# Up projection of the expert blocks: one bank and 512-column products instead of two banks and 256-column ones, with the gating multiply behind it

## What is computed

```python
def expert_block(args):
    xb_i, e = args
    h = jax.nn.silu(xb_i @ w_gate[e]) * (xb_i @ w_up[e])
    return h @ w_down[e]
```

## Time and profile before

| | us |
|---|---|
| median of 3 runs | 2057.61 |
| lowest, highest | 2056.06, 2059.81 |
| span of the profiled execution | 2054.1 |
| TensorE busy | 1895.9 (92%) |
| VectorE busy | 1034.9 (50%) |
| ScalarE busy | 832.3 (41%) |
| GpSimd busy | 283.8 (14%) |

### The profile page before, as it was taken

How to read it: one execution, slowest core, us unless ns; L and a number is a source line. 1 busy time by engine, 2 the same in 40 slices (tenths; PEclk the granted TensorE clock), 3 DMA queues, 4 the chain that set the end, 5 groups by cost and what they waited for, 6 DMA issues and landing times. The chain is left out here.

```text
span 2054.1 us, 28746 instructions
## 1 busy us (share of the span) xinstructions
PE 1895.9 (92%) x9892; PEld 1600.8 (78%) x9893; DVE 1034.9 (50%) x2051; ACT 832.3 (41%) x1564; POOL 283.8 (14%) x388
## 2 busy tenths in 40 slices
PE   6999999999999999999997764999999999999980
PEld 5788888888878888888885543888888888888870
DVE  4644455544454544555444654454456454546434
ACT  4333333333343333333323553444446454446423
POOL 2000000010000010000100202222222222222223
PEclk9999999999999999999997886999999999999995
DMA  6332333323342223522334575585566576656428
GB/s 213 123 100 85 139 140 132 103 92 135 123 145 96 90 83 131 173 77 95 103 123 166 169 250 168 149 268 162 155 224 218 169 264 191 184 174 215 142 53 340
DMA packets 173306, 316.24 MB, mean 154 GB/s; under 512 B 9757, under 2 KB 92701, under 8 KB 173226
## 3 DMA queue, kind: packets, MB, share of 16 engines
q1 hardware_dynamic: 155754, 255.07, 36.0%
q0 software_dynamic: 15120, 51.59, 10.1%
q10 hardware_dynamic: 2352, 8.52, 1.0%
HBM read 266.09 MB, written 49.07 MB: 153 GB/s over the span
## 5 line engine op out<-in xcount | busy, mean ns | idle before, releaser
L751 DVE TENSOR_TENSOR wl<-raw,wh 128x512 fp32r<-128x512 f32 x440 | 274.3, 685 | 207.2 <-ACT wh L573 205.3
L1597 PE MATMUL bank<-gu_hi,ex_hi 128*128 128x256 f32 (+1 forms) x960 | 310.5, 323 | 4.5 <-DVE gu_lo L1507 4.5
L60 PE MATMUL bank<-xT_hi,wh 128*128 128x512 f32 x768 | 301.0, 392 | 10.6 <-ACT ext L711 7.0
L1599 PE MATMUL bank<-gu_hi,ex_lo 128*128 128x256 f32 (+1 forms) x960 | 307.1, 320 | 0.0
L1598 PE MATMUL bank<-gu_lo,ex_hi 128*128 128x256 f32 (+1 forms) x960 | 306.9, 320 | 0.0
L62 PE MATMUL bank<-xT_hi,wl 128*128 128x512 f32 x768 | 299.4, 390 | 0.0
L61 PE MATMUL bank<-xT_lo,wh 128*128 128x512 f32 x768 | 299.3, 390 | 0.0
L573 ACT ACTIVATE wh<-raw 128x512 fp32r<-128x512 f32 x440 | 240.2, 619 | 99.5 <-PE bank L1140 49.9
L1597 PEld LDWEIGHTS bank<-gu_hi,ex_hi 128*128 128x128 f32 x960 | 183.2, 191 | 23.9 <-DVE gu_lo L1507 6.5
L1599 PEld LDWEIGHTS bank<-gu_hi,ex_lo 128*128 128x128 f32 x960 | 183.2, 191 | 13.3
L1598 PEld LDWEIGHTS bank<-gu_lo,ex_hi 128*128 128x128 f32 x960 | 183.5, 191 | 12.5
(11 more groups left out here) (239 smaller groups left out, 3258.0 us busy)
## 6 DMA issues: line engine op xcount, KB each, us to landing
raw<-in_w_in SPq DMA_DIRECT2D x70, 1024.0 KB
raw_gate_up<-in_w_gate SPq DMA_DIRECT2D x16, 2048.0 KB, 8.4
raw_gate_up<-in_w_up SPq DMA_DIRECT2D x16, 2048.0 KB, 13.4
raw_d<-in_w_down SPq DMA_DIRECT2D x16, 2048.0 KB, 13.0
raw<-in_w_out SPq DMA_DIRECT2D x20, 1024.0 KB
raw<-in_w_up_pool SPq DMA_DIRECT2D x20, 512.0 KB
raw<-in_w_up_gmlp SPq DMA_DIRECT2D x20, 512.0 KB
h<-in_x_prompt SPq DMA_DIRECT2D x16, 512.0 KB, 5.2
```

Of the source, the lines that this page charges most:

```text
L60: nc.tensor.matmul(out, lh, rh, start=(i == 0), stop=False)
L751: lo = lambda out, x, hi: tt(out, x, hi.bitcast(F32), ALU.subtract)
L1597: nc.tensor.matmul(out, a[0][:, ka, :], w[0][:, kw, cols], start=(n == 0), stop=False)
L1599: return nc.tensor.matmul(out, a[1][:, ka, :], w[0][:, kw, cols], start=False, stop=(n == total - 1))
```

## The change

The up projection goes into one bank (`bankU` is bank 1) with matmuls of 512 columns, in the same form as the gate projection. `u1_done` is gone. VectorE waits for `gu_done`, the end of the whole up projection, and then multiplies both halves of the hidden rows one behind the other. The first pair of transposes of the hidden rows moves behind the transposes of x. The second pair writes to bank 2, which is free now, instead of bank 0.

```diff
-    bankG, bankU, bankY = psum[0], psum[1:3], psum[3:5]
-    bankX, bankH = psum[5:7], [psum[7], psum[0]]
+    bankG, bankU, bankY = psum[0], psum[1], psum[3:5]
+    bankX, bankH = psum[5:7], [psum[7], psum[2]]
@@ VectorE, per_block
-                    dve.wait_ge(u1_done, j + 1)
-                    tt(hid[:, 0:256], bankU[0][:, 0:256], sg[:, 0:256], ALU.mult).then_inc(hid_ok, 1)
+                    dve.wait_ge(gu_done, j + 2)
+                    tt(hid[:, 0:256], bankU[:, 0:256], sg[:, 0:256], ALU.mult).then_inc(hid_ok, 1)
+                    tt(hid[:, 256:512], bankU[:, 256:512], sg[:, 256:512], ALU.mult).then_inc(hid_ok, 1)
                     down(0)
                     dve.wait_ge(hT_hi, 2 * j + 1)
                     hidden_low(0)
-                    dve.wait_ge(gu_done, j + 2)
-                    tt(hid[:, 256:512], bankU[1][:, 0:256], sg[:, 256:512], ALU.mult).then_inc(hid_ok, 1)
@@ TensorE, per_block
-                    early = 5 if first else 0
-                    up = lambda c, k: accumulate(bankU[c][:, 0:256], xT, k, gu, KD + k,
-                                                 slice(c * 256, (c + 1) * 256), k, KD)
...
                         pe.wait_ge(e_lo, SPLITS * e + KD + k + 1)
-                        last = up(0, k)
-                        if k < early:
-                            up(1, k)
-                    last.then_inc(u1_done, 1)
-                    for k in range(early, KD):
-                        last = up(1, k)
-                        if k == (6 if first else 4):
-                            pe.wait_ge(hid_ok, 2 * j + 1)
-                            hidden_transposed(0)
+                        last = accumulate(bankU[:, :], xT, k, gu, KD + k, slice(0, HALF), k, KD)
                     last.then_inc(gu_done, 1)
                     rows_of_x(16 * j + 32)
+                    pe.wait_ge(hid_ok, 2 * j + 1)
+                    hidden_transposed(0)
                     pe.wait_ge(y_read, 2 * j + 4)
                     pe.wait_ge(hT_lo, 2 * j + 2)
```

More of the change, by code:

```diff
@@ L1336, in phase_three @@
         ex_hi, ex_lo = sem("ex_hi"), sem("ex_lo")
-        g_done, u1_done, sg_ok, hid_ok = (sem(n) for n in ("g_done", "u1_done", "sg_ok", "hid_ok"))
+        g_done, sg_ok, hid_ok = (sem(n) for n in ("g_done", "sg_ok", "hid_ok"))
         gu_done = sem("gu_done")
```

## The result

The changed kernel takes 2097.24 us (median of 4 runs, 2096.84 to 2099.18) against 2058.71 for the kernel before (4 runs, 2056.06 to 2062.48): 1.0186 times as long, 95% interval 1.0171 to 1.0201. It is slower by 38.5 us. Medians and ratios in this document are of the fast executions alone: one of four in e3, one of twelve in e9 and in e10, and two of the 23 of the kernel before beside e9 and e10 fell in a slower state and are left out. The span of its profiled execution is 2095.9 us, 41.8 more than before.

A forecast was written before the change was run, and what follows sets the result against it. TensorE's queue was taken to bound the expert stage; profiled span 2054.1 + 37.8 net block loss + 3.5 from span to median = 2095.4 us. Range 2084 to 2116, the forecast's own 2088 to 2102.

The forecast's parts named there:

- The product step: Up projection: would take the gate's 5.48 us, gaining 0.51 us in a first block and 0.49 in a later one.
- The moved wait: Chain from hidden rows to down products: loses 1.30 us in a later block and 1.66 in a first one.
- What else moves: Rest of the block: the down projection keeps its distances, the next splits move along, and bank 2 costs nothing.
- The x960 of the signs: Profile sign in the up projection: its products show one shape, x960 at a step of 0.228.
- The sum: Expert stage: 24 x 0.81 and 16 x 1.15, together 37.8 us slower, giving 2095.4 us.
- The falling clock: Rival, TensorE's gaps: clock falls at 1.55 us each, 2157 us in all blocks, 2116 in one of three; chance 0.11.
- The larger gain: Rival, up projection: wide products gain more than the loss, from a step of 0.189 us, not slower; chance 0.03.
- The partly filled gap: Rival, hidden-to-down chain: links overlap, a block loses 0.8 us less, total near 2063 us; chance 0.02.

The follow-up runs named there:

- e3: Changed kernel with VectorE making the first low piece of the down weights ahead of its wait for the up projection, in first blocks; 2089.79 us, ratio 1.0163.
- e9: e6 with the first hidden piece transposed behind the fifth of eight transposes of x, and VectorE making two low down-weight pieces early; 2058.15 us, ratio 0.9985.
- e10: e8 with three steps of the up projection wide instead of four in later blocks; 2051.28 us, ratio 0.9966.
- e2: Changed kernel with the up projection again as 48 products of 256 columns in two banks, order and waits kept; 2110.33 us, ratio 1.0260.
- e1: Kernel before with only the first pair of hidden transposes moved behind the transposes of x; 2104.61 us, ratio 1.0226.
- e5: Changed kernel with four more VectorE multiplies of 256 columns into an unused tile ahead of the first hidden multiply; 2146.21 us, ratio 1.0425.
- e7: Kernel before with ScalarE splitting the last piece of the down weights ahead of its second hidden copy, in first blocks; 2054.88 us, ratio 0.9981.
- e8: e7 with the first four up projection steps of later blocks as 512-column products, the rest 256-column, VectorE adding both sums; 2055.85 us, ratio 0.9986.
- e6: Changed kernel with hidden rows cut 128 and 384, both transposed before down, early down-weight pieces, and ScalarE's copies of x last; 2064.87 us, ratio 1.0035.
- e4: Changed kernel with the first pair of hidden transposes ahead of the transposes of x; 2093.78 us, ratio 1.0173.

## Why the prediction was right

**The product step**: right, its size a little small. The gate and the up projection have one shape and the up projection takes the gate's time: from the first gate product to X a first block needs 10.91 (1366.81 to 1377.72) for 11.47 in the earlier trace rows, a gain of 0.56 for the 0.51 forecast. The gate of the first block of an expert, which served as the measure, has some steps of 0.23 to 0.24 us (5.48 in all), and the up projection of after goes at 0.227 throughout (5.45). Of the gain the narrow products were put at 0.27 a block, and e2 measured 0.31 and 0.32. The prediction calls them the smaller cause; 0.27 of 0.49 is already more than half, and this slip changed no term of the sum. The Trainium skill (TensorE: Matmul & The Clock Gate, Back-to-back issue gap) would, by its formula for the gap, have the merge of a pair save 2.5 ns; e2 shows 13. Setting the rows above the page was the right choice: by the page's figure the forecast would have been too high by 40 x 0.25 = 10 us, an estimate.

**The moved wait**: right in its chain, link by link. In the later block the links were forecast to start at X + 0.20, 0.79, 1.21 and 1.62 and down at 2.09; they start at 0.20, 0.87, 1.29, 1.71 and 2.23. Two terms were too small, and e1 shows both with the multiply far away: the eight transposes of x take 0.87 until a transpose follows, where the earlier trace rows showed 0.79 until a product, and the last hand-over, from VectorE's end to the product (1399.44 to 1399.54), takes 0.10 where I took 0.05 from the rows between other engines. The copy's link adds 0.01. That is 0.14 a block more; 0.05 more of gain and 0.02 less of down projection come off. Added to the 0.81 forecast this makes +0.88, and +0.89 is measured. In the first block the terms held: 0.20, 0.54, 0.87 and 2.00 for 0.20, 0.54, 0.88 and 2.01, and down at 2.66 for 2.67. VectorE's piece was the late link, and e3 showed it by taking it away. The net is +1.09 for +1.15.

**What else moves**: right. In the later block the second low part starts 2.29 behind down (1401.83 on the timeline) and the product that needs it 3.06 behind (1402.60), against 2.31 and 3.08 in the earlier trace rows; the down projection takes 6.05 and 5.79 us in first and later blocks, in before 6.05 and 5.81. The x960 of the signs is the number of up products; the profile has it over three lines, each with the gate's beside it, as x640. No wait on `hid` appears, and the idle time is 46.0 us where some 45 was written.

**The sum**: 24 x 0.89 + 16 x 1.09 = 38.8 for 37.8, and 38.5 between the medians. The time of 2097.24 lies 1.8 above the forecast of 2095.4. The errors of the later block add 1.9 and those of the first block take off 1.0, so a part of the closeness is that they cancel. Another 1.1 is the kernel before, whose median is 2058.71 with a fourth run and was 2057.61 when the forecast started from it. What is left is smaller than what moves ahead of the stage from run to run.

**The rivals.** The falling clock did not come: the granted clock is 1.00 over the stage with an idle stretch of 0.98 or 1.41 us in every block. The forecast gave it 0.11, and e5 shows that it was right to keep it: with 2.0 to 2.5 us of idle a block the clock fell twice, at 1.36 and 1.57 us a fall, where the earlier trace rows had given 1.55. The Trainium skill (TensorE: Matmul & The Clock Gate, A second HAM failure mode) has short idles between groups of products make the clock go up and down; the trace of after does not show it, and that of e5 shows it in 2 of 40 blocks. The larger gain would have needed a step under 0.189; it is 0.227. The partly filled gap did not come either: every hand-over of the chain between two engines comes behind the recorded end of its producer, by 0.04 to 0.10 us. The last one takes 0.24 in first blocks, with the register step between, and does so in e3 too, where the copy is the late link; no run takes the register step away, so that it is the cause is not shown.

## What to carry over

Merging products into wider ones buys little on TensorE (13 ns a pair here) and costs a dependency: everything that hung on the first half of the result now hangs on all of it. Before such a change, count the links from the result to the next product that needs it, and the work that TensorE has left to do meanwhile; where the plain change loses 38 us, a small first piece that is transposed early (e9) only wins the loss back, and making only the early part of the sum wide (e10) keeps a part of the gain, some 3 us against e7. The cover has to be long enough with every step counted: e8 lost nearly all that it had won because the hidden rows came 0.1 us late.

## What was not expected of the hardware

- VectorE and ScalarE take 0.29 and 0.28 us for 128 x 128 elements out of a bank (e9) and 0.42 and 0.38 for 128 x 256 (after): half the work saves only a quarter to a third. So a chain of small pieces still has its floor; in e6 the first piece of 128 columns brings down forward by 0.35 us in a later block.
- A product of 512 columns starts 0.03 us behind the last of a run of eight transposes, a further transpose 0.11 behind it, the step that the run itself has: 0.79 against 0.87 us for the eight, in all kernels of the study in which the one or the other follows without a wait. Whoever reads the length of a run of transposes from the product behind it takes it 0.08 too short, as the prediction did.
- A pair of transposes in the middle of the down projection costs 0.23 us in a later block (5.79 to 5.56 when e6 moves it out), although only 0.13 lie between its start and the next product's (1401.00 and 1401.13 in after): that product's own step is 0.32, not 0.23.
- TensorE can wait without a wait in the profile: e8 lost 0.16 us a later block with no line for it in the list of waits, because the idle time is counted from modelled ends. Only the distances between starts showed it.
- The first transpose behind an idle stretch holds the next one off by 0.16 us (e4) and 0.17 (e5), where the step of a run is 0.11.
